# Exponentials for sigmoid and gelu, two mixer panels exchanged, and the experts' last way down by halves

## The reference

```
first block:   x += parallel_mixer(rms_norm(x))        # dilated attention and retention, w_in, w_out
               x += memory_cross_attention(...)
               x += hierarchical_moe(rms_norm(x))      # 32 experts, top 2 of a group of 8
second block:  2 layers: x = ln(ALPHA*x + attention), x = ln(ALPHA*x + sqrelu_mlp(x))
```

```
proj = h @ w_in;  aq, ak, av, rq, rk, rv, rg = split(proj)
ret  = silu(rg) * head_group_norm(retention(rq, rk, rv))
expert e:  y = (silu(x @ w1[e]) * (x @ w3[e])) @ w2[e];  y_tok += gate * y
layer 0 attention:  gate = sigmoid(gate_logits)                      # 24 columns per token
                    h = gelu(blocks @ w1 + b1) (tanh form);  h @ w2  # compressed keys and values
```

## Time and profile before

| | |
|---|---|
| 3 runs | 2360.38, 2360.58 and 2364.09 us; median 2360.58 us |
| the profiled execution | 2362.44 us, its span (first to last instruction) 2361.1 us, granted clock 0.979 |
| busy, share of the span | PE 95%, DVE 43%, ACT 30%, POOL 4% |
| the chain of work that ended last | PE 82%, DMA 9%, DVE 4%, ACT 2% |
| bytes | 370 MB, of it 201 MB of experts' weights |

### The profile page before, as it was taken

One profiled execution on the slowest core, in us unless ns is written; L12 is line 12 of the kernel. 1 busy time (PEld: TensorE's weight loads), 2 busy tenths in 40 slices (PEclk: granted clock), 3 DMA queues, 4 the chain that ended last, 5 costly groups with the idle time before them and its releaser, 6 DMA issues.

```text
span 2361.1 us, 28318 instructions
## 1 busy us (share of the span) xinstructions
PE 2236.7 (95%) x11771; PEld 1647.0 (70%) x11771; DVE 1020.7 (43%) x1858; ACT 716.6 (30%) x1249; POOL 103.1 (4%) x109
## 2 busy tenths in 40 slices
PE   8999899979989889899889999999999999999998
PEld 6866687864433334388656788888878777888887
DVE  5336465342322232443567553234432466433335
ACT  4325354320000000132456233133132462331330
POOL 2101001000000000000000000000000000000001
PEclk9999999989999999999989999999999999999999
DMA  5233343268999999732110232322142201332320
GB/s 194 93 110 108 103 161 109 80 227 365 426 427 427 427 427 427 322 109 87 37 54 2 90 125 90 103 93 93 51 156 89 72 1 59 107 103 90 107 90 36
DMA packets 106740, 370.27 MB, mean 157 GB/s; under 512 B 15168, under 2 KB 20672, under 8 KB 94320
## 3 DMA queue, kind: packets, MB, share of 16 engines
q1 hardware_dynamic: 103584, 361.58, 40.8%
q0 software_dynamic: 3024, 6.83, 0.9%
HBM read 368.32 MB, written 4.19 MB: 158 GB/s over the span
## 4 chain that ended last, share of the span: by engine, by line
PE 82%; DMA 9%; DVE 4%; ACT 2%; issue 1%; POOL 0%; SPq 0%; DVEq 0%; ACTq 0%; POOLq 0%
PE PB L457 56%; PE PB L1934 9%; PE PB L474 5%; PE PB L776 4%; PE PB L467 3%; DMA FL_raw<-in_w_exp_gate 3%; PE PB L668 3%; DMA FH_raw<-in_w_exp_gate 3%; DMA Z<-in_w_exp_gate 1%; DMA W_raw<-in_w_exp_down 1%; PE PB L792 1%; PE PB L673 1%; ACT nsp L702 1%; DMA scratch_h<-Z 1%; DMA X<-in_x 0%
## 5 line engine op out<-in xcount | busy, mean ns | idle before, releaser
L457 PE MATMUL PB<-W,FH 128*128 128x512 f32 (+1 forms) x1792 | 556.0, 392 | 6.1 <-DVE FL L837 5.2
L449 DVE TENSOR_TENSOR W<-R,W 128x2048 fp32r<-128x2048 f32 (+1 forms) x128 | 291.3, 2277 | 606.9 <-ACT W L441 606.9
L441 ACT ACTIVATE W<-R 128x2048 fp32r<-128x2048 f32 (+1 forms) x128 | 243.4, 1902 | 648.8 <-PE PB L457 642.0
L457 PEld LDWEIGHTS PB<-W,FH 128*128 128x128 f32 x1792 | 330.9, 189 | 73.4 <-DVE FL L837 6.3
L457 PE MATMUL PB<-W,hid 128*128 128x512 f32 x1536 | 349.4, 390 | 0.0
L457 PE MATMUL PB<-W,FL 128*128 128x512 f32 (+1 forms) x896 | 348.2, 389 | 0.0
L457 PEld LDWEIGHTS PB<-W,hid 128*128 128x128 f32 x1536 | 288.4, 188 | 59.5
L457 PE MATMUL PB<-FH,W 128*128 128x512 f32 (+1 forms) x1152 | 324.5, 367 | 4.5 <-DVE FL L562 4.5
L457 PEld LDWEIGHTS PB<-FH,W 128*128 128x128 f32 x1152 | 208.7, 189 | 40.5 <-issue 5.0
L457 PE MATMUL PB<-FL,W 128*128 128x512 f32 (+1 forms) x576 | 210.9, 366 | 0.0
L457 PEld LDWEIGHTS PB<-W,FL 128*128 128x128 f32 x896 | 169.2, 189 | 34.7
(11 more groups left out here) (337 smaller groups left out, 2587.4 us busy)
## 6 DMA issues: line engine op xcount, KB each, us to landing
R<-in_mlp_w_up SPq DMA_DIRECT2D x32, 1024.0 KB, 5.3
R<-in_mlp_w_down SPq DMA_DIRECT2D x32, 1024.0 KB, 5.1
Z<-in_w_exp_down SPq DMA_DIRECT2D x14, 2048.0 KB, 29.5
Z<-in_w_exp_up SPq DMA_DIRECT2D x13, 2048.0 KB, 35.2
R<-in_w_exp_gate SPq DMA_DIRECT2D x11, 2048.0 KB, 33.8
W_raw<-in_w_exp_up SPq DMA_DIRECT2D x10, 2048.0 KB, 31.5
R<-in_w_exp_up SPq DMA_DIRECT2D x9, 2048.0 KB, 30.9
R<-in_w_in SPq DMA_DIRECT2D x12, 1024.0 KB, 5.3
```

What stands on the lines that cost most here:

```text
L441: k.A.e.activation(w.splits[w.split_of[u]][0][:, 0:m], w.rows(u), ACT.Copy).then_inc(*w.hi.tick(u))
L449: k.V.e.tensor_tensor(wl[:, 0:m], w.rows(u), wh[:, 0:m].bitcast(F32), ALU.subtract).then_inc(*w.lo.tick(u))
L457: ins = te.matmul(bank, l, r, start=(start and n == 0), stop=(stop and n == len(terms) - 1), skip_group_check=True)
```

## The change

- **Mixer.** The units of panels 4 and 5 change places: panel 4 is now the gates `rg` (Silu on ACT), panel 5 the values `rv` (DVE). The decays move from panel 2 to panel 5.
- **Experts, way down.** A product takes one bank and one half of the 1024 columns at a time; `halved` tells ACT that the first half is done, so `y_hi` of half 0 can start there. `give_back`, `add` and the waits go by halves. `mark` n-1 comes in round n, before `y_lo`, and not in round n+1.
- **Experts, last pair.** The two last loads come in four parts, both experts' left columns first (`sp_load_last`). PE goes: turn 15, down 15 left, `give_back` 14, down 15 right, `give_back` 15. Both cuts (`a0`, `a0+1`) stand behind everything else on ACT and DVE.
- **Flag.** Rounds 0 to 2 (`BEGUN = 3`) are issued, then every engine waits for `over` and reads the flag into its register, then the other rounds follow. The branch stays where it was.
- **Gates.** ACT gives exp(-x); DVE adds 1 and takes the reciprocal once for all four tiles, ahead of the attention.
- **Gelu.** DVE makes u = max(x + 0.044715 x^3, -50) in three operations behind the bias; ACT takes exp(-2 sqrt(2/pi) u), now at the step's `score` stage; DVE adds 1, takes the reciprocal and multiplies by x at `weigh`.

```diff
+BEGUN = 3
     panels("w_in", a["w_in"][0, :, 0:3072])
+    units[8:12] = units[10:12] + units[8:10]
@@ act_mix (dve_mix alike)
-        if p == 2:
+        if p == 5:
             act_decay(k)
...
-            elif p == 5:
+            elif p == 4:
                 ae.activation(k.rg[:, i, :], bank[:], ACT.Silu, scale=k.rstat["mix", i]).then_inc(
@@ sp_load_last, new
+    loads = x.loads[-2:]
+    for half in range(2):
+        at = slice(512 * half, 512 * half + 512)
+        for side, (which, n, _) in enumerate(loads):
+            u = len(x.loads) - 2 + side
+            if half == 0:
+                k.Y.wait_ge(*x.multiplied.at(*x.loads[x.prior[u]]))
+            src = k.a["w_exp_down"][0][2 * n + side].rearrange("(p k) n -> p k n", k=4)[:, :, at]
+            done = x.landed[x.slot_of[x.loads[u]]].tick(u) if half else x.half_landed[side].tick()
+            k.Y.e.dma_start(x.weights(which, n, side)[:, :, at], src).then_inc(*done)
@@ pe_blocks, end of the rounds
+    bank = k.banks.take(T, ("y", m - 1, 0), x.y_v.at(m - 1, 0), hold=True)
+    T.wait_ge(*x.at_out.at(m - 1))
+    if x is k.x1:
+        for side in range(2):
+            T.wait_ge(*x.half_landed[side].at())
...
+    product(m - 1, "down", k.aT[(m - 1) % 2], 4, bank, 0, False)
+    give_back(m - 2, 0)
+    give_back(m - 2, 1)
+    k.banks.release(("y", m - 1, 0))
+    bank = k.banks.take(T, ("y", m - 1, 1), x.y_v.at(m - 1, 1))
+    landed(m - 1, "down")
+    product(m - 1, "down", k.aT[(m - 1) % 2], 4, bank, 1, True)
+    give_back(m - 1, 0)
+    give_back(m - 1, 1)
@@ act_blocks
         if n:
-            A.wait_ge(*x.multiplied.at("down", n - 1, 1))
-            if n >= 2:
-                A.wait_ge(*x.summed.at(n - 2, 3, 1))
             for half in range(2):
+                if n >= 2:
+                    A.wait_ge(*x.summed.at(n - 2, 3, half))
+                A.wait_ge(*(x.multiplied.at("down", n - 1, 1) if half else x.halved.at(n - 1)))
                 ae.activation(k.y_hi[:, 512 * half:512 * half + 512], k.banks["y", n - 1, half][:],
@@ act_even
-                ae.activation(k.gates[:, i, :], bank[:, 256:280], ACT.Sigmoid).then_inc(*k.gates_out.tick(i))
+                ae.activation(k.gates[:, i, :], bank[:, 256:280], ACT.Exp, scale=-1.0).then_inc(*k.gates_out.tick(i))
@@ act_even_attention
-            elif kind == "biased" and what == "weigh":
+            elif kind == "biased" and what == "score":
                 A.wait_ge(*k.dve_step.at("biased"))
-                ae.activation(k.hrow, k.hrow, ACT.Gelu_apprx_tanh).then_inc(*k.act_step.tick("gelu"))
+                ae.activation(k.hscr, k.hscr, ACT.Exp, scale=-2.0 * math.sqrt(2.0 / math.pi)).then_inc(*k.act_step.tick("gelu"))
@@ new
+def dve_hidden_biased(k):
+    V, ve, x, u = k.V, k.V.e, k.hrow, k.hscr
+    V.wait_ge(*k.pe_step.at("windows", 3))
+    V.settle(ve.tensor_tensor(x, k.banks["hidden",][:, 0:256], k.b1, ALU.add))
+    V.settle(ve.scalar_tensor_tensor(out=u, in0=x, scalar=0.044715, in1=x, op0=ALU.mult, op1=ALU.mult))
+    V.settle(ve.scalar_tensor_tensor(out=u, in0=u, scalar=1.0, in1=x, op0=ALU.add, op1=ALU.mult))
+    ve.tensor_scalar(u, u, -50.0, None, ALU.max).then_inc(*k.dve_step.tick("biased"))
+def dve_hidden_gelu(k):
+    V.wait_ge(*k.act_step.at("gelu"))
+    V.settle(ve.tensor_scalar(u, u, 1.0, None, ALU.add))
+    V.settle(ve.reciprocal(u, u))
+    ve.tensor_tensor(k.hrow, k.hrow, u, ALU.mult).then_inc(*k.dve_step.tick("gelu"))
@@ dve_even_attention
+    V.wait_ge(*k.gates_out.at(3))
+    V.settle(ve.tensor_scalar(k.gates, k.gates, 1.0, None, ALU.add))
+    V.settle(ve.reciprocal(k.gates, k.gates))
@@ engines
     for e in k.all:
         e.wait_ge(*k.dve_step.at("over"))
+    if not counting:
+        many = nc.values_load(k.over_i[0:1, MORE:MORE + 1], engines=ENGS, min_val=0, max_val=1)
+    pe_blocks(k, k.x1, BEGUN, NPAIR + 1)
...
-        many = nc.values_load(k.over_i[0:1, MORE:MORE + 1], engines=ENGS, min_val=0, max_val=1)
         with nc.If(many > 0):
             overflow(k)
```

More of the change, by code:

```diff
@@ L1923, in turn, with landed @@
             flips(k, bank, [k.xg[n % 3][:, 4 * half + c::8] for c in range(4)]).then_inc(*x.fed_turned.tick(n, half))
-    def product(n, which, lhs, rows, banks):
+    def landed(n, which):
         for side in range(2):
@@ L1954, in pe_blocks @@
             T.wait_ge(*x.fed_v.at(n))
-            product(n, "gate", k.xT[n % 2], 8, [bank])
+            landed(n, "gate")
+            product(n, "gate", k.xT[n % 2], 8, bank, 0, True)
         if n == 0 and x is k.x1:
@@ L1982, in feed @@
         ae.activation(k.xT[n % 2][:, 0:512], k.banks["fed", n, 0][:], ACT.Copy).then_inc(*x.fed_a.tick(n))
-    if x is k.x1:
-        A.wait_ge(*k.rowed.at("moe", 3))
-        A.wait_ge(*k.dve_step.at("places", "rows"))
-    feed(0)
-    for n in range(m + 1):
+    if begin == 0:
+        if x is k.x1:
+            A.wait_ge(*k.rowed.at("moe", 3))
+            A.wait_ge(*k.dve_step.at("places", "rows"))
+        feed(0)
+    for n in range(begin, end):
         if n:
@@ L2047, in dve_blocks @@
         if n >= 2:
-            add(n - 2)
-        if x is k.x1 and n == m:
-            dve_cut(k, k.start["after"])
+            add(n - 2, 0)
+            add(n - 2, 1)
         if n < m:
@@ L2064, in dve_blocks, with pool_blocks @@
                              ALU.subtract).then_inc(*x.y_v.tick(n - 1, half))
-    add(m - 1)
-    if x is k.x1:
-        dve_cut(k, k.start["after"] + 1)
-def pool_blocks(k, x):
-    m = x.pairs
+    if end == m + 1:
+        add(m - 1, 0)
+        add(m - 1, 1)
+        if x is k.x1:
+            dve_cut(k, k.start["after"])
+            dve_cut(k, k.start["after"] + 1)
+def pool_blocks(k, x, begin, end):
     def gather(n):
@@ L2077, in gather @@
                                  bounds_check=S - 1, oob_is_err=False).then_inc(*x.gathered[n % 3].tick(n))
-    for n in range(m):
+    for n in range(begin, end):
         gather(n)
-def pool_experts(k):
-    k.G.wait_ge(*k.dve_step.at("places", "rows"))
-    pool_blocks(k, k.x1)
 def sp_experts(k):
     x, a0 = k.x1, k.start["after"]
-    for u in range(9, len(x.loads)):
+    for u in range(9 + BEGUN, len(x.loads) - 2):
         sp_load(k, x, u)
+    sp_load_last(k, x)
     for slot, upto in ((1, a0 + 2), (4, a0 + 4)):
@@ L3290, in pool_first @@
     pool_router(k)
-    pool_experts(k)
+    k.G.wait_ge(*k.dve_step.at("places", "rows"))
+    pool_blocks(k, k.x1, 0, BEGUN)
 def sp_first(k):
@@ L3298, in sp_first @@
     sp_router(k)
-    sp_experts(k)
+    for u in range(9, 9 + BEGUN):
+        sp_load(k, k.x1, u)
 def pe_rest(k):
```

149 lines of the change are left out of this document (83 added, 66 removed).

## The result

| | before | after |
|---|---|---|
| runs | 20, median 2361.05 us (2357.54 to 2364.58) | 20, median 2366.45 us (2358.6 to 2371.71) |
| profiled execution | 2362.44 us, span 2361.1 | 2368.23 us, span 2366.9, granted clock 0.978 |
| ratio | | 1.0020, 95% interval 1.0014 to 1.0026 |

The change made the kernel 5.4 us slower; the forecast was 4.9 us faster, and the range ended at 2360.0. One execution among the experiments (e3, 3742.48 us at a granted clock of 0.555) is left out everywhere. The lines of the code moved: `group` is L469 (was 467), the turn L476 (474), the projection's product L459 (457), the experts' product L1952 (1934), the cuts L443 and L451 (441, 449), the features' halves L554 and L564 (552, 562).

A forecast was written before the change was run, and what follows sets the result against it. DMA was taken to bound the experts' stretch, and elsewhere PE (95% busy) and the waits between its products. Tail 4.4 + gates 1.0 - gelu 0.5 + mixer 0 = 4.9 us: 2360.58 to 2355.7 us, range 2352.0 to 2360.0.

The forecast's parts named there:

- The tail, 4.4 us: Experts' last pair to the second block's projection: reordered halves and earlier flag read gain 4.4 us, bounds 2 to 5.5.
- The transposes decide, at about 1005.05 against 1009.43: Behind PE's branch: the transposes' end (1004.95), not DVE's subtractions (1004.3), sets the projection's start; 4.4 us gained.
- The gates, 1.0 us: Gates: a 1.28 us table load leaves the chain, 1.0 us gained, bounds 0.8 to 1.3; new DVE operations cost 0.
- The gelu, -0.5 us: Gelu: two table loads go, but PE's products wait for ACT's later copy; 0.5 us lost, bounds 0.3 gained to 1.5 lost.
- The operation of the same size: Gelu's reciprocal of 256 columns, not in the trace: taken as 0.42 us from an operation of that size, bounds 0.2 to 0.8.
- rival 4: Gelu costs 2 us or more because ACT's wait pushes every tile behind it; 2358 us and above, chance 0.08.
- The mixer, 0: Mixer's reordered panels gain nothing, since the bias table sets the chain; Exp's table load goes or falls earlier.
- The flag's load and the rounds, 0: Experts' rounds: reading the flag there costs 0, bound 0.5 us; marks and halves cost 0 where DMA decides.
- Rival 1: Tail: DVE's two cuts and own branch hold the gain to 3.2 us or less; 2357.4, up to 2358.5 us, chance 0.18.
- rival 2: Tail: the branch's stall leaves with the register load, transposes start at 996.7; 2353.9 or 2353 us, chance 0.16.
- Rival 3: Experts' last weights: the 2 KB pieces land late, at 994, costing 5.3 us; 2361.0 us, chance 0.06.
- 0.04 for slower: Whole kernel: chance given to a slower result, from late 2 KB pieces above their price or something not seen.

The follow-up runs named there:

- e3: Kernel after, plus 16 PE instructions in the part that isn't run and the banks' rotation of the kernel before; ratio 0.9988 to the kernel before.
- e1: Kernel after with 8 transposes (16 PE instructions) added in the part that isn't run; ratio 1.0016 to the kernel before.
- e5: e3 with the gelu done as in the kernel before; ratio 0.9983 to the kernel before.
- e7: e3 with 106 transposes instead of 8 in the part that isn't run; the 32 transposes ran in one piece, no total time given.
- e12: Kernel before with only the experts' part and the gates' exponential, plus both layout edits of e3; ratio 0.9984 to the kernel before.
- e8: e5 without ACT's wait for the mixer's last panel ahead of its first exponential; ratio 0.9984 to the kernel before.
- e4: Kernel before with 116 transposes (232 PE instructions) added in the part that isn't run; ratio 1.0024 to the kernel before.
- e2: Kernel after with the rotation of the PSUM banks moved on by 6, as in the kernel before; 3.7 us under the kernel after.
- e6: e3 with the gelu's reciprocal replaced by a minimum with 1.0, which leaves the gelu out; 3.8 us under e3.

## Why the prediction was wrong

The sum was 4.4 + 1.0 - 0.5 + 0. Against it:
- **The tail, 4.4 us: the mechanism was right, the step behind it failed.** `give_back` between the halves, the branch 3.7 us earlier (both relative to the weights' landing), its duration of 5.7 to 6.7 us kept, DVE not in the way (but for e1): all as written. With the layout put right it gave 3.2 us (e3), 3.9 (e5, e7, e12) and 4.2 (e8); the size hangs on the branch, 6.58 us in e3 and 5.90 in e5. The step that failed is "The transposes decide, at about 1005.05 against 1009.43". (The paragraph's own 1004.95 would make its 4.4 us 4.5.) It took for granted that what stands behind the branch runs as before, because no edit touched it. Two properties of it changed without an edit: the place of its first instruction in PE's stream (+3.2 us, e1 and e4) and the bank from which it starts (+2.3 us at the projection, +1.1 us at the forgetting gates, less 0.5 in the gates' stretch: after against e2). Both could have been had without a run: the instructions that the diff adds and removes ahead of the target, and the number of banks taken while one is held. The price of the first could not; the trace of before shows no second hole.
- **The gates, 1.0 us: right.** 1.3 in the first comparison, of which some 0.4 is the banks'; in e3, with the banks as before, the distance from the last turn of the first tile to that of the next falls from 3.42 to 2.42 us. The two new DVE operations were mis-sized here too (0.75 us for the reciprocal against a bound of 0.4) and cost nothing only because DVE's wait had room for them.
- **The gelu, -0.5 us: mis-sized.** The reciprocal of 128x256 takes 1.75 us, four times what was taken. "The operation of the same size" was the wrong neighbour; the upper bound should have come from the reciprocal's own growth with its columns; the trace had 0.18 us for 4 and 0.20 us for 8 columns, too close together for more than the direction. The form cost 2.6 to 3.8 us in time, 1.0 of it direct. That is rival 4's price (chance 0.08), but not its mechanism, ACT's wait: the direct cost is the reciprocal's, and how the rest comes about stays open, since the granted clock of the stretch scatters by as much.
- **The mixer, 0: right,** by the mechanism given (the bias table decides). One sentence was wrong: the load of the exponential's table came later, not earlier, because two waits now stand ahead of ACT's first exponential, and the load is held by one of them.
- **The flag's load and the rounds, 0: right.** Nothing in the rounds moved by more than 0.6 us (the stretch from the first expert's product to the last landing is 422.4 before, 421.9 to 422.7 in the others).
- Rival 1 didn't happen in the kernel after, where DVE's cuts ended at 1004.5 and PE's hole lasted until 1005.80 (in e1, without the hole, they were in the path). Nor did rival 2: the stall stayed with the branch when the load had gone. Rival 3 neither: the right halves had landed when PE came to them.

Of the chances, 0.04 for slower was the real fault. The case "a second stall, or another bank, behind the branch" wasn't among the rivals, and it held more than the whole of the loss: -3.2 - 1.0 for what the change meant to do, +3.2 + 2.3 + 1.1 - 0.5 for the layout, and +2.6 to 3.8 for the gelu make +4.5 to +5.7; measured 5.4. The agreement is looser than it looks: the first terms are read from single profiles, the gelu's from medians, and e1 shows that the terms of the layout don't add in time. By its own marks the prediction was wrong where it said so: PE waited for DVE's subtractions far beyond 1005, though for the bank that they emptied and not because DVE was late; and the branch took 6.06 us, just outside its 5 to 6.

## What to carry to other kernels

- An edit ahead of a taken branch moves everything behind it in the instruction stream. Look whether a hole of "issue" stands within some 4 us behind the target; instructions in a part that isn't run are enough to move it. The instruction packets of the DMA view tell whether it is a fetch.
- A helper that hands out banks in turn couples places far apart: an edit that takes one more, or holds one, shifts who waits for whom in every later stage. Compare the bank numbers at the joints, not only the order of instructions.
- Bound an operation that the trace doesn't show by its own kind at another size before using another kind at the same size; and before a difference of a microsecond is read from two profiles, ask a third one how far that stretch scatters.

## What the runs showed of the hardware that was not expected

- RECIPROCAL on DVE: 1.75 us for 128x256 and 0.75 us for 128x96, against 0.41 us for a TENSOR_TENSOR of 128x256 and 0.20 us for a reciprocal of 8 columns: about 6.3 ns more a column.
- PE's taken branch cost 5.69 to 6.73 us in 14 profiles of the same branch. If the end of a block of instructions follows within 10 instructions, PE stops again, for 2.5 to 3.8 us, until 1.3 to 1.5 us behind the end of a 16 KB instruction packet (four kernels).
- An ACT table load can be held by a wait of the function behind it: with two waits ahead of the first exponential, the load began behind the second (156.97); with one, it went ahead of it, as soon as ACT was free (155.69, and 140.06 in e8).
- The granted clock differs between kernels in stretches whose instructions are the same. Between the last panel and the experts e2 and e6 needed 371.3 and 371.7 us where all others needed 376.1 to 377.1; around 170 us they ran at full clock and the kernel before at 0.76. What sets this off wasn't found. Five microseconds, as much as the whole effect that was looked for:
```profile
165.00:185.00 20.00, 20.00 (x146) 13.06 (x146) 13.24 (x32) 7.06 (x15) 1.48 (x3) 1.00 0.17 54
```
```profile
165.00:185.00 20.00, 20.00 (x101) 12.06 (x102) 9.93 (x26) 6.28 (x13) 0.00 (x0) 0.76 0.17 53
```
The first is e2, the second the kernel before.
